# A two-block transformer kernel: in the forgetting attention, both heads' score products are issued together and the two mask products behind them

## What is computed

```python
def forgetting_attention(x, w_q, w_o, k, v, c):
    q = (x @ w_q).reshape(B, S, B_HEADS, B_HEAD_DIM).astype(jnp.float32) * (B_HEAD_DIM ** -0.5)
    for i in range(S // Q_BLOCK):
        q0 = i * Q_BLOCK
        k_end = q0 + Q_BLOCK
        dist = jnp.arange(q0, k_end)[:, None] - jnp.arange(k_end)[None, :]
        decay = c[:, :, q0:k_end, None] - c[:, :, None, :k_end]
        logits = jnp.einsum('bqhd,bkhd->bhqk', q[:, q0:k_end], k[:, :k_end]) + decay
        logits = jnp.where(dist >= 0, logits, NEG_INF)
        p = jax.nn.softmax(logits, axis=-1)
        outs.append(jnp.einsum('bhqk,bkhd->bqhd', p, v[:, :k_end]))
```

## Time and profile before

| | |
|---|---|
| runs | 2779.33 us median of 3 (2778.93 to 2779.91) |
| the profiled execution | 2774.35 us, its span 2772.5 us |
| busy share of the span | PE 94%, weight loads (PEld) 77%, DVE 53%, ACT 25%, POOL 58% |
| granted TensorE clock, mean | 0.968 of full speed |
| chain that ended last, by engine | PE 73%, DVE 7%, issue 1%, ACT 1% |
| memory traffic | 229.17 MB, mean 83 GB/s |
| forgetting attention | about 2083 to 2345 us of the span |
| differential attention | about 1396 to 1600 us of the span |

### The profile page before, as it was taken

How to read it: one execution, slowest core, us unless ns; L and a number is a source line. 1 busy time by engine, 2 the same in 40 slices (tenths; PEclk the granted TensorE clock), 3 DMA queues, 4 the chain that set the end, 5 groups by cost and what they waited for, 6 DMA issues and landing times.

```text
span 2772.5 us, 37315 instructions
## 1 busy us (share of the span) xinstructions
PE 2615.4 (94%) x12877; PEld 2127.4 (77%) x12895; DVE 1463.2 (53%) x2056; ACT 705.3 (25%) x1251; POOL 1607.9 (58%) x1548
## 2 busy tenths in 40 slices
PE   8879899898999999999999799999999999999998
PEld 6668778787877878888777577888876776788886
DVE  5676676453433533320457757784164445687722
ACT  2233333100123221110224433331021222333300
POOL 6534454574544667777644357888653332588874
PEclk9989898999999999999999999999999999999999
DMA  4332232232222333332312122333222221233321
GB/s 138 119 84 80 69 103 76 69 96 68 69 63 63 109 89 97 95 99 95 114 59 67 40 64 84 97 96 99 81 73 65 66 69 31 69 98 95 98 96 64
DMA packets 235781, 229.17 MB, mean 83 GB/s; under 512 B 15808, under 2 KB 228288, under 8 KB 235664
## 3 DMA queue, kind: packets, MB, share of 16 engines
q1 hardware_dynamic: 212224, 204.72, 24.7%
q10 hardware_dynamic: 23440, 22.82, 2.9%
HBM read 222.67 MB, written 4.82 MB: 82 GB/s over the span
## 4 chain that ended last, share of the span: by engine, by line
PE 73%; DVE 7%; issue 1%; ACT 1%; DVEq 0%; ACTq 0%
PE PS L605 56%; PE PS L599 5%; PE PS L676 2%; PE AUX L904 2%; PE AUX L953 1%; PE AUX L853 1%; PE AUX L943 1%; DVE AUX L1849 1%; DVE half_acc L1396 1%; DVE opA_lo L1378 1%; PE AUX L958 1%; PE AUX L872 1%; PE AUX L701 1%; PE AUX L862 0%; DVE bstat L1932 0%
## 5 line engine op out<-in xcount | busy, mean ns | idle before, releaser
L563 POOL TENSOR_SCALAR whi<-raw 128x512 fp32r<-128x512 f32 x772 | 553.5, 717 | 1072.7 <-issue 532.1
L565 POOL TENSOR_TENSOR wlo<-raw,whi 128x512 fp32r<-128x512 f32 x772 | 1055.8, 1368 | 64.4
L605 PE MATMUL PS<-opA_hi,whi 128*128 128x512 f32 x1872 | 749.6, 400 | 17.0 <-DVE opA_lo L1378 5.7
L605 PE MATMUL PS<-opA_lo,whi 128*128 128x512 f32 x1872 | 736.0, 393 | 0.0
L605 PE MATMUL PS<-opA_hi,wlo 128*128 128x512 f32 x1872 | 735.5, 393 | 0.0
L605 PEld LDWEIGHTS PS<-opA_hi,whi 128*128 128x128 f32 x1872 | 356.0, 190 | 103.2 <-issue 9.8
L605 PEld LDWEIGHTS PS<-opA_hi,wlo 128*128 128x128 f32 x1872 | 355.8, 190 | 76.1
L605 PEld LDWEIGHTS PS<-opA_lo,whi 128*128 128x128 f32 x1872 | 356.1, 190 | 71.7 <-issue 1.0
L1873 DVE SCALAR_TENSOR_TENSOR facc<-fu,vec,facc 128x512 f32<-128x512 f32 x176 | 202.2, 1205 | 52.7 <-ACT facc L1267 52.7
L599 PE MATMUL PS<-whi,opA_hi 128*128 128x256 f32 x704 | 210.6, 299 | 1.4 <-DVE y_ssm L1614 1.0
L599 PE MATMUL PS<-whi,opA_lo 128*128 128x256 f32 x704 | 203.0, 288 | 0.0
(11 more groups left out here) (302 smaller groups left out, 3569.1 us busy)
## 6 DMA issues: line engine op xcount, KB each, us to landing
raw<-in_w_in_dram SPq DMA_DIRECT2D x184, 256.0 KB, 2.7
raw<-in_ffn_w_in_dram SPq DMA_DIRECT2D x176, 256.0 KB, 2.7
raw<-in_ffn_w_out_dram SPq DMA_DIRECT2D x88, 256.0 KB, 2.6
raw<-in_a_w_qkv_dram SPq DMA_DIRECT2D x48, 256.0 KB, 2.7
raw<-in_w_ffn_gate_dram SPq DMA_DIRECT2D x44, 256.0 KB, 2.7
raw<-in_w_ffn_up_dram SPq DMA_DIRECT2D x44, 256.0 KB, 2.7
raw<-in_w_ffn_down_dram SPq DMA_DIRECT2D x44, 256.0 KB, 2.6
acs_row<-acs_dram ACTq DMA_DIRECT2D x16, 512.0 KB, 5.7
```

Of the source, the lines that this page charges most:

```text
L563: nc.gpsimd.tensor_scalar(whi[slot][:], raw[raw_slot][:], 1.0, 1.0, ALU.mult, ALU.mult).then_inc(w_high, 1)
L565: nc.gpsimd.tensor_tensor(wlo[slot][:], raw[raw_slot][:], whi[slot][:].bitcast(F32), ALU.subtract).then_inc(slab_split, 1)
L605: last = nc.tensor.matmul(psum_fm(key, panel, m), a, b[:, k, :], start=k + n == 0, stop=k == total - 1 and n == 2)
```

## The change

In `scores(u)` the loop over the two heads now issues only the two score products. A second loop of `2 * fox` rounds issues the mask products behind both. Number, operands and banks of the products are the same, and the semaphore is still raised by the last of them.

```diff
                         rows = slice(64 * e, 64 * e + 64)
                         last = nc.tensor.matmul(AUX[:, e, 0:width], q2[j % 2][rows, hh, q0:q0 + P], k2[j % 2][rows, hh, 0:width],
                                                 start=True, stop=True)
-                        if fox:
-                            last = nc.tensor.matmul(AUX[:, e, q0:width], ident_bf[:], mask1[:, 2 * S + P:2 * S + 2 * P],
-                                                    start=False, stop=True, skip_group_check=True)
+                    for e in range(2 * fox):
+                        last = nc.tensor.matmul(AUX[:, e, q0:width], ident_bf[:], mask1[:, 2 * S + P:2 * S + 2 * P],
+                                                start=False, stop=True, skip_group_check=True)
                     last.then_inc(s2_done, 1)
```

## The result

The changed kernel takes 2749.55 us (median of 4 runs, 2744.58 to 2752.16), against 2779.13 for the kernel before (2776.35 to 2779.91): ratio 0.9896, 95% interval 0.9882 to 0.9909, 29.6 us less. A second set of runs gave 2749.74 against 2778.79; one execution of the changed kernel in it, 4770.1 us at a granted clock of 0.82 against 0.967 to 0.970 in the others, fell into a slow state and is not counted. The forecast was 2753.3, with a range of 2748 to 2761.

The account below looks back on a forecast made before the run. TensorE was taken as the one full engine in the forgetting attention. Net 26.7 + 0.8 for low clock - 0.9 - 0.2 for waits = 26.4, said as 26 us: 2779.3 - 26 = 2753.3 us, range 2748 to 2761.

Parts of the forecast that it names:

- What bounds it, and the mechanism: Forgetting attention: TensorE is the one full engine; without the mask between, two heads' scores run side by side.
- Net 26.7 us from the rows: Forgetting attention's 32 units: 28.6 us removed from scores to slab, 1.9 us added for the second masks.
- g: Distance from a unit's first mask to its second: taken as 0.06 us, bounded by 0.04 and 0.16.
- Low clock. Gain 0.8: Some forgetting-attention score products ran at low clock; the half that goes away carries about 0.8 us of the excess.
- What is not given back: 0.9 and 0.2: Savings turned into waiting: 0.9 us at unit 24 behind VectorE, 0.2 at unit 27's V for the copied probabilities.
- The range: 2748 to 2761 us for the whole run, the forecast's own bounds being 2748 to 2760.
- the slab at low clock (1.4): Range term: one slab more or less at the low clock in the attention, 1.4 us either way.
- Rival A: Softmax chain on VectorE takes up the slack at 14 places, 11.7 us less: gain 14 us, 2765; chance 0.10.
- Rival B: Pairs do not run side by side; only half-to-full row changes are saved: 3.2 us, 2776; chance 0.03.
- a = 0.42 us: Time from a unit's scores to its mask, before the change: 0.42, 0.63, 0.84, 1.05 us by width.
- Rival C: Thinner TensorE work makes the clock fall more often in the attention: slower, 2803 if 100 us; chance 0.02.

Follow-up runs that it names:

- 512-key experiment: Pairing of the change only for the eight 512-key units, the others in the order of the kernel before: 2768.96 us against 2778.67 (ratio 0.9974).
- same rows in the old order: Kernel before, with both heads' score products in the forgetting attention on partitions 0 to 63: 2779.85 us against 2778.79 (ratio 1.0004).
- same rows in the new order: Changed kernel, with both heads' score products in the forgetting attention on partitions 0 to 63: 2765.35 us against 2778.57 (ratio 0.9949).
- the moved slabs in both attentions: Changed kernel, with the missing slab put ahead of V instead of behind it, in both attentions: 2754.65 us (ratio 0.9919 to the kernel before).

## Why the prediction was right

**What bounds it, and the mechanism**: right. The pair took what a single took, the group fell to 26.2 us, and in the 512-key experiment six of eight units returned 1.14 to 1.16 us for 1.15.

**Net 26.7 us from the rows**: right to the hundredth at the distances of all four widths, with g = 0.055 to 0.06. The 81 ns of the page TensorE: Matmul & The Clock Gate of the Trainium skill (Part 2, Back-to-back issue gap) would have made each unit 0.02 us longer; the measured distance decides for the lower value.

**"Low clock. Gain 0.8"**: mis-sized, the largest error of the sum: it came to 5.7 us. I counted only the score products that had run at low clock. The clock itself changed, for everything in those stretches. In stretches (us, busy and count per engine, clock, DMA share), the second trace of the kernel before:

```profile
2084.00:2092.00 8.00, 6.33 (x18) 2.97 (x20) 3.74 (x11) 1.45 (x7) 1.40 (x2) 0.60 0.21 65
2156.00:2168.00 12.00, 11.28 (x49) 8.18 (x47) 4.66 (x12) 2.54 (x9) 1.96 (x3) 0.72 0.08 23
...
2296.00:2320.00 24.00, 20.20 (x86) 13.98 (x85) 12.39 (x31) 7.11 (x20) 1.34 (x2) 0.79 0.01 2
```

and the changed kernel:

```profile
2084.00:2092.00 8.00, 5.87 (x33) 4.01 (x32) 2.48 (x6) 0.67 (x3) 4.38 (x5) 1.00 0.56 181
2156.00:2168.00 12.00, 12.00 (x63) 9.36 (x62) 6.14 (x14) 3.21 (x9) 5.72 (x6) 1.00 0.15 45
2272.00:2296.00 24.00, 18.65 (x101) 13.28 (x99) 13.76 (x35) 7.89 (x21) 1.89 (x2) 0.86 0.04 12
```

Before, the engine was at its lower level (1.2 GHz, which is 0.50 of full) for a while at the attention's start, again near 2160 us, and before the end; of the three the changed kernel keeps the last. A stretch of T us at a mean clock c has 2 x (1 - c) x T at the low level: 20 and 24 us in the traces of before (in 4 us stretches), 6.8 in both of the change. At half clock the difference of 14 to 17 us is worth at most 7 or 8 us, less what falls into waits. What it was worth stands in the steps from the start of one unit's scores to the next. Of the 32 steps 26 lie at full clock in all four traces; they saved 19.1 us (means of two traces each) where the distances of the scores give 21.9. The other six (units 0, 1, 2, 10, 27 and 28, counted by the scores that begin the step) met a low stretch in one trace at least; they saved 10.2 us where the distances give 4.8. That is 5.4 us more, and 5.7 with the 0.3 us of waiting at unit 26's `V` (below) that stands in one of them. Unit 10 shows it best: its step took 10.0 and 11.6 us before, and the same step eight units later, at full clock, 8.5.

**"What is not given back: 0.9 and 0.2"**: right in kind, too small (3.0 us). From unit 24's transposes to the next (2291.58 and 2297.57 are the scores behind them, before) it was 5.99 us before and is 5.98 now: the 0.94 us are lost as said. Unit 27's `V` waits 0.22 as said; that of unit 26 waits 0.29, which I had let pass because that unit stood at low clock. What I missed is unit 28, 5.92 us before and 6.30 now, though its scores are 0.94 shorter. VectorE there in the changed kernel, and three of the same lines before:

```profile
2300.39 0.29 DVE L1938 COPY pT<-AUX 128x128 f32<-128x128 f32 x1 [2.37 <-PE AUX L943]
2300.60 0.15 DVE L1941 RECIPROCAL bstat<-bstat 128x2 f32<-128x2 f32 x1
2301.11 1.74 DVE L1376 TENSOR_TENSOR opA_lo<-oT,opA_hi 128x512 fp32r<-128x512 f32 x1 [0.35 <-ACT opA_hi L1319]
2302.77 1.13 DVE L1923 SCALAR_TENSOR_TENSOR sc<-negc,ccol,AUX 128x384 f32<-128x384 f32 x2
2303.93 0.95 DVE L1932 TENSOR_REDUCE bstat<-sc 128x2 f32<-128x768 f32 x1
2304.92 0.59 DVE L1934 TENSOR_SCALAR bstat<-bstat 128x2 f32<-128x2 f32 x1
...
2322.78 1.73 DVE L1376 TENSOR_TENSOR opA_lo<-oT,opA_hi 128x512 fp32r<-128x512 f32 x1 [0.35 <-ACT opA_hi L1319]
2324.43 1.12 DVE L1923 SCALAR_TENSOR_TENSOR sc<-negc,ccol,AUX 128x384 f32<-128x384 f32 x2
2326.57 0.17 DVE L1934 TENSOR_SCALAR bstat<-bstat 128x2 f32<-128x2 f32 x1
```

The decay is added 2.79 us after the transposes began (2299.98 to 2302.77), as before (2321.64 to 2324.43): the low part (line 1376) holds VectorE until then, not the scores. Lost: 0.94, and 0.4 more since line 1934 took 0.59 us instead of 0.17. And unit 30's transposes came 5.11 us after the scores ahead of them where it had been 6.05, so of the 1.15 us of those scores 0.2 were lost too. Sum 0.94 + 0.22 + 0.29 + 1.33 + 0.2 = 3.0 us, where I had 1.1. Together 26.7 + 5.7 - 3.0 = 29.4, against 29.3 measured. The two errors, 4.9 us too little for the clock and 1.9 too little for the waits, leave the forecast of 26.4 just 3 short; that they have opposite signs is luck, not foresight.

**The range** of 2748 to 2761 held, but its lower edge doesn't follow from its terms: the slab at low clock (1.4), the spread of the runs (1) and g at 0.04 (0.6) take 2753.3 down to 2750.3 only, and the measured 2749.55 lies below that. The term that was missing there is again the clock, for which 1.4 us either way was too narrow.

**Rival A** held at two places (units 24 and 28), not at fourteen. **Rival B** did not come true, but its price was wrong: "only the changes between half and full rows, 3.2 us" would have been 32 x 0.30 = 9.6 us by distances, and measured 13 with the clock. I had counted the visible gap from mask to scores (0.16) and not the tail that each score product pays before a mask can start: of a = 0.42 us at 128 keys some 0.20 don't grow with the width (0.63, 0.84, 1.05 add 0.21 per 128 keys). One such tail and the 0.16 - 0.06 make the 0.30. The page TensorEngine Tiling (Key Properties) of the Trainium skill says that a change of tiling mode drains the engine; the 0.30 us a unit for two changes fewer agree with it. The page gives no price; it would only have warned that the visible gap need not be all. **Rival C** went the other way: the clock rose. (Its text says that the trace before shows no low level after pairs. That was wrong: in the differential attention, where all scores are in pairs, the clock is 0.68 from 1560 to 1576 us.) In the four traces with the heads apart in most or all units (before twice, 512-key units alone, same rows in the old order) the clock of the attention is 0.96, with the same rows in the new order 0.97. With both heads side by side in every unit it is 0.98 to 0.99 in eight traces, and 0.96 in a ninth, the moved slabs in both attentions, which has the low stretch at the attention's start again (0.72 from 2092 to 2104 us). So pairing goes with a higher clock and doesn't ensure it; whether it is the cause, or the stretches only fall otherwise because everything stands elsewhere in time, stays open, and no run was made to separate these.

## What to carry to other kernels

In this kernel, products of half the rows ran side by side only where nothing of full rows came between; look at the distances between starts (0.52 against 1.04 us here), not at the engine's busy share, which stayed at 94%. Where a small full-row product like a mask belongs to each of them, issue it behind all of them, or make it half-row too where that computes the same (here it left out the mask for half of the queries). When TensorE's queue gets shorter, look next at what VectorE does in the units where it was just hidden, and at where the cover (a slab) stands: here moving it was worth another 8 us in one attention and cost about 7 us of waiting in the other.

## What the runs showed of the hardware

A half-row mask of one head doesn't hold back the other head's half-row scores: with half-row masks in the old order, all four score records started before the first head's mask (2103.78 us), although that mask stands ahead of the second head's scores in the queue.

VectorE and GpSimd got into each other's way. The low part of line 1376 takes 0.68 us at least, and 1.74 where GpSimd's split (line 565) ran from 2301.03 to 2302.30 us, starting just ahead of it. Over the whole first traces of both kernels, 26 of its 32 runs took 0.68 or 0.69 us; the other six (0.90 to 1.74) are those that began while line 565 had 0.3 us or more still to run. Line 1934, 0.17 us in 50 of 64 runs in the changed kernel, took 0.59 where line 563 ran from 2304.88 to 2305.50, having begun 0.04 us earlier. With both masks twice, GpSimd began 0.06 us after VectorE at the same place (2298.53), and line 1934 took its 0.17:

```profile
2298.47 0.17 DVE L1934 TENSOR_SCALAR bstat<-bstat 128x2 f32<-128x2 f32 x1
```

In both slow cases VectorE ended soon after GpSimd had. The page SBUF — State Buffer of the Trainium skill (SBUF: two separate sides) says that the two share a port pair which whoever is first holds for its whole instruction, VectorE only for an instruction with two inputs in SBUF or in a two-port mode. Line 1376 has two such inputs and agrees. Line 1934 has one; its times look the same, but the trace doesn't show in which mode it ran.

Of TensorE's three low stretches in this attention the changed kernel has one, in both of its traces: 14 to 17 us less at the low level, though no wait was taken away. I had expected none of it, or the opposite; its cause stays open.
